# A gate's modulation summed on GpSimd and spread by a product with ones, in a transformer kernel on one core

## What is computed

```python
def adaln(cvec, w, b):
    m = jax.nn.silu(cvec) @ w + b
    return jnp.split(m, 3, axis=-1)

h = rms_norm(x, pre_g[i]) * (1.0 + scale) + shift
hc = rms_norm(xc, pre_g[i]) * (1.0 + cscale) + cshift
...
x = x + gate * rms_norm(y, post_g[i])
if not last:
    xc = xc + cgate * rms_norm(yc, post_g[i])
```

## Time and profile before

| | |
|---|---|
| time, 3 runs | 805.94 us median (805.93 to 806.41) |
| profiled execution, its own time | 805.69 us |
| its span, first to last instruction | 803.7 us |
| TensorE busy | 789.2 us |
| DVE, ScalarE busy | 505.1 us, 393.8 us |
| GpSimd busy | 42.9 us |

### The profile page before, as it was taken

How to read it: one execution, slowest core, us unless ns; L and a number is a source line. 1 busy time by engine, 2 the same in 40 slices (tenths; PEclk the granted TensorE clock), 3 DMA queues, 4 the chain that set the end, 5 groups by cost and what they waited for, 6 DMA issues and landing times. The chain is left out here.

```text
span 803.7 us, 11013 instructions
## 1 busy us (share of the span) xinstructions
PE 789.2 (98%) x4108; PEld 626.2 (78%) x4108; DVE 505.1 (63%) x873; ACT 393.8 (49%) x728; POOL 42.9 (5%) x55
## 2 busy tenths in 40 slices
PE   9999999999999999999999999999999999999998
PEld 5577787777777778777778877887788888888886
DVE  3474545225768776669856667799887645556454
ACT  3541323235878673575636646735245533343431
POOL 0120000000001001002100001300000000000000
PEclk9999999999999999999999999999999999999999
DMA  9974552355000037337432016883216655466521
GB/s 338 388 239 153 210 192 80 147 210 200 11 1 1 1 119 275 105 105 274 172 105 75 31 64 211 300 308 125 79 53 210 208 180 187 158 201 214 176 91 52
DMA packets 71303, 125.56 MB, mean 156 GB/s; under 512 B 2714, under 2 KB 28652, under 8 KB 71124
## 3 DMA queue, kind: packets, MB, share of 16 engines
q1 hardware_dynamic: 70208, 122.47, 43.8%
q0 software_dynamic: 512, 1.18, 0.5%
q10 hardware_dynamic: 532, 1.21, 0.5%
HBM read 123.79 MB, written 1.06 MB: 155 GB/s over the span
## 5 line engine op out<-in xcount | busy, mean ns | idle before, releaser
L822 PE MATMUL psum<-w_hi,act_hi 128*128 128x512 f32 (+1 forms) x712 | 289.6, 407 | 3.0 <-DVE w_lo L1973 1.0
L823 PE MATMUL psum<-w_lo,act_hi 128*128 128x512 f32 (+1 forms) x752 | 291.9, 388 | 0.0
L824 PE MATMUL psum<-w_hi,act_lo 128*128 128x512 f32 (+1 forms) x712 | 276.8, 389 | 0.0
L1948 DVE TENSOR_TENSOR w_lo<-raw,w_hi 128x2048 fp32r<-128x2048 f32 (+1 forms) x70 | 157.9, 2262 | 103.5 <-ACT w_hi L1369 103.4
L1369 ACT ACTIVATE w_hi<-raw 128x2048 fp32r<-128x2048 f32 (+1 forms) x74 | 139.9, 1895 | 71.2 <-PE psum L824 36.6
L822 PEld LDWEIGHTS psum<-w_hi,act_hi 128*128 128x128 f32 x712 | 133.7, 188 | 45.8 <-issue 17.3
L823 PEld LDWEIGHTS psum<-w_lo,act_hi 128*128 128x128 f32 x752 | 141.6, 188 | 25.4 <-issue 1.0
L824 PEld LDWEIGHTS psum<-w_hi,act_lo 128*128 128x128 f32 x712 | 133.7, 188 | 28.6
L1916 POOL TENSOR_TENSOR rstd<-ms,half_neg 128x1 f32<-128x1 f32 (+3 forms) x38 | 36.3, 957 | 557.6 <-DVE ms L1989 557.6
L1526 ACT ACTIVATE sc<-psum,nmax 128x512 f32<-128x512 f32 (+1 forms) x64 | 36.7, 585 | 24.2 <-DVE nmax L2196 24.2
L1451 ACT ACTIVATE sc<-psum 128x512 f32<-128x512 f32 (+1 forms) x62 | 32.4, 525 | 16.2 <-PE psum L925 8.7
(11 more groups left out here) (272 smaller groups left out, 991.1 us busy)
## 6 DMA issues: line engine op xcount, KB each, us to landing
raw<-in_a_w_in SPq DMA_DIRECT2D x16, 1024.0 KB, 9.8
raw<-in_ada_w SPq DMA_DIRECT2D x16, 1024.0 KB, 5.3
raw<-in_w_out SPq DMA_DIRECT2D x12, 1024.0 KB, 5.1
raw<-in_w_gate SPq DMA_DIRECT2D x22, 512.0 KB, 4.1
raw<-in_w_up SPq DMA_DIRECT2D x22, 512.0 KB, 5.2
raw<-in_w_down SPq DMA_DIRECT2D x11, 1024.0 KB, 5.0
raw<-in_b_w_in SPq DMA_DIRECT2D x10, 1024.0 KB, 7.7
raw<-in_w_in SPq DMA_DIRECT2D x10, 1024.0 KB, 5.9
```

Of the source, the lines that this page charges most:

```text
L822: pe.matmul(oh, x_hi, hi, start=(k == 0), stop=False)
L823: pe.matmul(o[:, 0:n], x_hi, lo, start=False, stop=False)
L824: mm = pe.matmul(oh, x_lo, hi, start=False, stop=(k == KT - 1))
L1948: ins = dve.tensor_tensor(rest, weights, hi.bitcast(F32), ALU.subtract)
```

## The change

The four gate parts are no longer multiplied on TensorE. GpSimd takes them from the raw ring: `gate_block` multiplies row block k by the block's column of silu (a value for each partition) and adds it to a total of 128x512. The totals, one for each part and condition, lie in `gate0`, and the product in `scaled`. A half is released (`s_sumused`) with its last product. `gate_row` then multiplies the total by a 128x128 matrix of ones, which adds up the partitions and spreads the sum. In the first projection the blocks stand behind GpSimd's small loads, in the second between its powers. The gate rows of in1 come after (1, 1) and (2, 2). The four pairs "norm1c" get banks 4 to 7. post_g of layer 0 is loaded by SP into kT with the other loads of that place and no longer by GpSimd. `sel` shrinks to two columns, `taken` moves into memory that another buffer shares. The diff, without these last declarations:

```diff
-BESIDE_IN0 = {(0, 3): ("ada0g", 0), (1, 1): ("ada0g", 1)}
-BESIDE_IN0.update({(2 + c, 1 if c < 3 else 0): ("ada1", c) for c in range(4)})
+BESIDE_IN0 = {(2 + c, 1 if c < 3 else 0): ("ada1", c) for c in range(4)}
 COLUMNS_IN0 = {(2 + c, 3 if c < 3 else 2): c for c in range(4)}
-BESIDE_IN1 = {(0, 0): 4, (1, 1): 5}
-GATE_IN1 = {(1, 0): 0, (2, 1): 1}
+SUMMED = [("ada0g", 0, (0, 1)), ("ada0g", 1, (0, 1)), ("ada1", 4, (0,)), ("ada1", 5, (0,))]
+GATE_IN1 = {(1, 1): 0, (2, 2): 1}
...
@@ -79,6 +80,8 @@
         for t in range(NT):
             if (c, t) in BESIDE_IN0:
                 plan += both(*BESIDE_IN0[(c, t)])
+        if c < 2:
+            plan += both("ada0g", c)
     for stage, chunks in (("out0", 2), ("in1", 5), ("out1", 2), ("in2", 6), ("out2", 2)):
         for c in range(chunks):
...
@@ -218,14 +221,13 @@
         put(("out0", 1, XT + t), 6 + t)
     norm("norm1")
     units("in1", range(3))
+    put(("gate1", 0, 0), 6)
     for pair in range(HALF_KT):
-        put(("norm1c", pair), 4 + pair % 2)
+        put(("norm1c", pair), 4 + pair)
     for c in range(3):
         for t in gemm_tiles("in1", c):
             put(("turn1", c, t), 2 + t)
-    for c in range(2):
-        put(("ada1", 4 + c, 0), 6 + c)
-        put(("gate1", 0, c), 6 + c)
+    put(("gate1", 0, 1), 7)
     for p in range(XT * HEADS):
         put(("s1", p), 2 + p % 2)
         put(("t1", p), 6)
...
+        def gate_sum(stage, c, s):
+            part = c if stage == "ada0g" else c - 4
+            return gate0[:, s, part * COLS:(part + 1) * COLS]
+        sum_no = {key: n for n, key in enumerate((stage, c, s) for stage, c, conds in SUMMED for s in conds)}
         def mod_rows(l, c):
             if l == 0:
                 return mrow[:, c * COLS:(c + 1) * COLS]
-            return sc[:, 5 + c % 2, :] if c < HALF_KT else mrow0g[:, (c - 4) * COLS:(c - 3) * COLS]
+            return sc[:, 5 + c % 2, :]
         k_flat = kT[:].rearrange("p h n -> p (h n)")
         gain2, gain3 = gate0[:, 1, :], q_flat[:, D:2 * D]
...
@@ -562,8 +572,11 @@
         emptied, firsts = {}, 0
+        summed_halves = [(stage, c, h) for stage, c, _ in SUMMED for h in range(2)]
         for n, (stage, c, h) in enumerate(loads):
-            if not stage.startswith("ada"):
+            if (stage, c, h) in summed_halves:
+                emptied[n] = (s_sumused, summed_halves.index((stage, c, h)) + 1)
+            elif not stage.startswith("ada"):
                 emptied[n] = released[half_no[(stage, c, h)]]
             elif h == 0:
                 firsts += 1
@@ -645,6 +658,7 @@
                     load(k_flat[:, 0:D], a["ada_b"][0, 2 * D:3 * D].partition_broadcast(P), s_par1)
                     load(k_flat[:, D:2 * D], a["ada_b"][1, 2 * D:3 * D].partition_broadcast(P), s_par1)
                     load(k_flat[:, 2 * D:3 * D], a["post_g"][1].partition_broadcast(P), s_par1)
+                    load(k_flat[:, 3 * D:4 * D], a["post_g"][0].partition_broadcast(P), s_par1)
                 if loads[n] == ("out1", 0, 0):
                     sp.wait_ge(s_res, NT)
...
@@ -855,18 +869,18 @@
                 name = (f"mod{l}", c)
                 o = begin(name)
                 for blk in range(HALF_KT):
-                    mm = pe.matmul(o[:, 2 * blk:2 * blk + 2], rows[:, blk * P:(blk + 1) * P], sel[:, :, 0],
+                    mm = pe.matmul(o[:, 2 * blk:2 * blk + 2], rows[:, blk * P:(blk + 1) * P], sel[:],
                                    start=True, stop=True)
                 mm.then_inc(bank_full(name), 1)
             def gate_row(l, s, c):
-                rows = mod_rows(1, 4 + c) if l else mrow0g[:, c * COLS:(c + 1) * COLS]
-                pe.wait_ge(*moved(("ada1", 4 + c, 0) if l else ("ada0g", c, 0)))
+                key = ("ada1", 4 + c, s) if l else ("ada0g", c, s)
+                pe.wait_ge(s_ones, 1)
+                pe.wait_ge(s_summed, sum_no[key] + 1)
                 name = (f"gate{l}", s, c)
                 o = begin(name)
-                pe.matmul(o, sel[:, s, :], rows,
-                          start=True, stop=True).then_inc(bank_full(name), 1)
+                pe.matmul(o, ones[:], gate_sum(*key), start=True, stop=True).then_inc(bank_full(name), 1)
             def norm(stage, ks=range(KT)):
                 tiles = norm_tiles[stage]
@@ -1073,9 +1087,6 @@
                     turn(("turn1", *units[n - 2]), 4 if units[n - 2][0] < 2 else 2)
                 if n == len(units):
                     gemm_unit("in1", 3, 0, ks=range(0, 5))
-                if n < len(units) and units[n] in BESIDE_IN1:
-                    for h in range(2):
-                        ada_half("ada1", BESIDE_IN1[units[n]], h)
                 if n < len(units) and units[n] in NORM_IN1:
                     norm("norm1c", NORM_IN1[units[n]])
                 if n < len(units) and units[n] in GATE_IN1:
...
@@ -1930,6 +1935,38 @@
                              (w_ukv[:, 0, :], a["w_uk_2"][0]), (w_ukv[:, 1, :], a["w_uv_2"][0]),
                              (relb[:], a["rel_bias_2"])):
                 pool.dma_start(dst, src).then_inc(s_late, 16)
+            def gate_block(stage, c, conds, k):
+                n = load_no[(stage, c, k // HALF_KT)]
+                if k % HALF_KT == 0:
+                    pool.wait_ge(landed[n % RAW], landed_at[n])
+                w = raw_view(n)[:, k % HALF_KT, :]
+                for s in conds:
+                    total, value = gate_sum(stage, c, s), cols[:, 8 * s + k:8 * s + k + 1]
+                    pool.wait_ge(*seq.last)
+                    used = s_sumused if k % HALF_KT == HALF_KT - 1 and s == conds[-1] else s_g
+                    seq.note(pool.tensor_scalar(scaled[:] if k else total, w, value, None, ALU.mult).then_inc(used, 1), used)
+                    if k:
+                        done = s_summed if k == KT - 1 else s_g
+                        pool.wait_ge(*seq.last)
+                        seq.note(pool.tensor_tensor(total, total, scaled[:], ALU.add).then_inc(done, 1), done)
+            pool.wait_ge(s_cst, 1)
+            for stage, c, conds in SUMMED[0:2]:
+                for k in range(KT):
+                    gate_block(stage, c, conds, k)
+            powers_through(("norm1", 2))
+            pool.wait_ge(s_res, NT - 1)
+            for key, (stage, c, conds), ks in ((("qk1", 0, 0), SUMMED[2], range(0, 3)), (("qk1", 0, 1), SUMMED[2], range(3, 5)),
+                                               (("post0", 3), SUMMED[2], range(5, KT)), (("qk1", 1, 0), SUMMED[3], range(0, 2)),
+                                               (("norm1", 3), SUMMED[3], range(2, 4)), (("qk1", 1, 1), SUMMED[3], range(4, KT))):
+                powers_through(key)
+                for k in ks:
+                    gate_block(stage, c, conds, k)
             powers_through(("ka", XT - 1))
             powers_through(("norm3", XT - 1))
...
@@ -2415,8 +2453,6 @@
                     if (c, t) == (0, 1):
                         post_mean(0, 3)
                         residual(0, 3)
-                    elif (c, t) == (1, 1):
-                        gates1(0)
                     return
                 r, buf = rs(key), sc[:, 5 + n % 2, w * P:2 * w * P] if t < XT else rot_buf(nm)
                 dve.wait_ge(s_vals, t + 1)
```

More of the change, by code:

```diff
@@ L316, in block_kernel @@
             rest_q = parts.enter_context(nc.sbuf_tensor("rest_q", [P, NT * HEADS, P], F32R))
+            taken = parts.enter_context(nc.sbuf_tensor("taken", [P, XT, 256], F32R))
         xs = sb("xs", [P, NT, D])
@@ L326, in block_kernel @@
         zbuf = sb("zbuf", [P, NT, D])
+        scaled = sb("scaled", [P, COLS])
         gate0 = sb("gate0", [P, 2, D])
@@ L330, in block_kernel @@
         ident_r = sb("ident_r", [P, P], F32R)
-        taken = sb("taken", [P, XT, 256], F32R)
         vecs = sb("vecs", [P, P])
@@ L335, in block_kernel @@
         cstat = sb("cstat", [P, KT, 32])
-        sel = sb("sel", [P, 2, P])
+        sel = sb("sel", [P, 2])
+        ones = sb("ones", [P, P])
         mod = sb("mod", [P, 2, 2, KT, 2])
@@ L437, in block_kernel @@
         s_res, s_yret = sem("residual_ready"), sem("retention_head_done")
-        N_CIN, N_VEC, N_LATE = 3, 4, 10
-        mrow0g = gate0[:, 0, :]
+        s_sumused, s_summed, s_ones = sem("summed_half_used"), sem("gate_sum_ready"), sem("ones_ready")
+        N_CIN, N_VEC, N_LATE = 3, 4, 9
+        def gate_sum(stage, c, s):
+            part = c if stage == "ada0g" else c - 4
+            return gate0[:, s, part * COLS:(part + 1) * COLS]
+        sum_no = {key: n for n, key in enumerate((stage, c, s) for stage, c, conds in SUMMED for s in conds)}
         def mod_rows(l, c):
@@ L1510, in unit0 @@
                     stage, part = BESIDE_IN0[before]
-                    if stage == "ada0g":
-                        move(mrow0g[:, part * COLS:(part + 1) * COLS], (stage, part, 0))
-                    else:
-                        move(mod_rows(1, part), (stage, part, 0), wait_for=("mod1", part - 2) if part >= 2 else None)
```

(15 more changed lines are left out.)

## The result

The changed kernel takes **889.76 us**, median of 4 runs (889.63 to 890.77), against 805.93 for the kernel before beside it: a ratio of 1.1042, interval 1.1022 to 1.1061. It is 83.8 us slower, where 18.7 was forecast; the range ended at 845. The profiled execution has a span of 887.8 us.

The account below looks back on a forecast made before the run. The prediction took TensorE, busy 98% of the span, as the bound, fed through a ring of six raw buffers. First projection +8.5, second +11.2 and banks -1.0 made +18.7 on 805.69: 824.4 us, range 799 to 845.

Parts of the forecast that it names:

- Product 0.54 us, addition 1.08: GpSimd's assumed time per 128x512 operation in both projections, from a memset's growth per column, doubled for the addition.
- upper pair: Dearer GpSimd prices, from a power's fixed cost plus the memset's slope: product 0.86 us, addition 1.32.
- Blocking 13.4 us: First projection: DVE's two-input time, four splits and five pairs of rotation ends, charged to GpSimd's sums.
- Rival 2: No blocking between DVE and GpSimd, operations at 0.54 and 1.08: 806.5 us, either side of no change; chance 0.12.
- First projection +8.5: Net us there: TensorE 12.6 late for chunk 3's second half, held by GpSimd in the ring, less 4.1 saved.
- Second projection +11.2: TensorE's wait for chunk 2's second half, ready at 395.6 against use at 384.40, the 4.0 saved already included.
- costs nothing more: Second projection: the gate's product on TensorE adds no wait, its sum being there by 387.
- Late powers 0 to 6: Second projection: GpSimd's last blocks delay tile (2,0)'s powers, 0 to 6 us; taken as nothing, hidden by another delay.
- Banks -1.0: Second projection: the fourth pair of context's transposes no longer waits for a bank, 1.0 us gained.
- Four parts, -8.1: Four gate parts leave TensorE, 2.0 us each, 8.1 in all, about 4.1 in each projection.
- Slow operations: Rival 3: GpSimd's operations at 0.86 and 1.32 us, late powers costing 6: 851 us; chance 0.15.
- Rival 1: GpSimd keeps up, averaging under 0.8 us per operation, blocking included: 802.2 us, 796.6 at best; chance 0.18.

Follow-up runs that it names:

- product_tt: Changed kernel with GpSimd's product written as an operation with two tensor inputs, the value broadcast along the row: 866.08 us.
- spaced: Kernel before with only the first projection's two gate parts on GpSimd, two-input product, loaded behind chunks 1 and 6: 807.54 us.
- free_raw: Changed kernel, but GpSimd reads ones instead of the raw halves, and a half counts as released once landed: 835.56 us.
- one_part: Kernel before with gate part 0 alone on GpSimd, two-input product, loaded behind the first projection's chunk 1; part 1 on TensorE: 803.48 us.
- attn: Kernel before with gate part 0 alone on GpSimd, two-input product, loaded behind the first projection's last chunk and summed beside attention: 807.77 us.
- second_alone: Kernel before with the change in the second projection alone, four banks included; first projection's gate parts on TensorE: 839.57 us.
- power_first: second_alone with the power of (2, 0) ahead of GpSimd's last four blocks and that of (2, 1) ahead of the last two: 831.14 us.
- banks_row: Kernel before with the four banks for context's features and the second gate row after tile (2, 2), nothing else: 809.07 us.
- awake: Kernel before with the first projection's change and four banks, plus matmuls on old data where TensorE stands longest: 862.43 us, against 862.39 without those matmuls.
- both_mended: Changed kernel with the two-input product and the powers of (2,0) and (2,1) ahead of GpSimd's last four row blocks: 865.02 us.

## Why the prediction was wrong

**In the first projection the mechanism held and its sizes did not; in the second the path was wrong.** SP's loads stood behind GpSimd in the order forecast, chunk 2's two halves and chunk 3's, and nothing after; TensorE stood for w_lo there. Of the 65.1 us between forecast and result, about 41.8 are the first projection (50.3 in place of 8.5) and 23.4 the second with its banks (33.6 in place of 10.2).

- *Product 0.54 us, addition 1.08.* This step failed most. Measured 1.56 and 1.27 undisturbed. Both prices came from how a memset grows with columns, which reads nothing. For 32 products and 28 additions that is 85.5 us in place of 47.5. The choice between two readings of the earlier trace rows, the memset's 0.9 ns a column and the power's 0.16 us, was made by what seemed alike; the measured 1.56 for 512 columns is over three times the memset's slope and a fiftieth of the power's, and my upper pair, 0.86 and 1.32, covered the addition and not the product. The estimate by the Trainium skill (GPSIMD Engine Reference, Elementwise side-by-side cycle accounting), 1.12 for the addition, was 12% low: near. That a product with one tensor input costs more than an addition with two is against its rule of thumb (the same page, Engine selection, calls one-input work "roughly line-rate" and only two-input work slow), and product_tt shows that it is the form of the instruction: the same product took 1.04 with two inputs.
- *Blocking 13.4 us.* GpSimd was busy 94.1 us between 55.9 and 155.7, 8.6 more than 85.5: less than forecast, in a longer stretch, because DVE now stood for the ring as well (67.5 us before its splits, from 54 to 180). In spaced, where DVE does not stand for the ring, the same 8.6 fall on 45.6 us (busy 43.2 against 34.6), close to the 13.4 in 60 that I had summed from the earlier trace rows. Rival 2, no blocking, falls by the product at 85.25. What I had not priced is the other direction: at nothing in the first projection in free_raw and one_part, at 1.2 us of waits there in spaced, and at 4.8 and 4.7 us in attention (attn, spaced).
- *First projection +8.5.* 50.3, and the chain of the prediction gives it when the sizes are put right. The second half of chunk 3 was released at 154.3 (the product at 152.69 ends), not 114.5: 37.8 later by the operations, 5.6 by 59 gaps of just under 0.1 that I had not priced, 1.2 by the later start, less 4.8 of blocking: 39.8. With the 9.6 of landing, rounding and split that is 163.9, and TensorE restarted at 163.79. So it is 12.6 + 39.8 - 4.1 = 48.3, and the low clock behind that last stall, 2 us, makes 50.3. The stalls before it (12.29 for chunk 2's *first* half, where the prediction had "some 2 us") are parts of the same sum, not additions to it.
- *Second projection +11.2, the sum "costs nothing more".* 33.6, by another road. The ring's hold was there and hidden (free_raw). The sum came at 393.2 on the clock of before (443.22 less 50.04, by which SP's loads of in1 had shifted, 396.58 for 346.54), not 387; and I compared it with TensorE's time of the next ring wait, though the gate's product stands before that in TensorE's order, at 378.6. 393.2 - 378.6 = 14.6. With the forecast's own 387 the product would have stood 8.4, so this is an error of the path and not only of a size. The sum of the stretch: 29.4 for the two long waits, 3.1 for w_lo and the rotation, some 5 of low clock behind them (an estimate from the granted clocks), less 4.1 for the parts and 1.0 for the old bank wait, 32.4; the last 1.2 is left open.
- *Late powers 0 to 6, taken at nothing.* 14.7. The shadow that was to hide it, the ring's wait at tile (2, 0), was 1.9 us long (until 451.18) and lay earlier in the chain, behind the sum's wait. second_alone less power_first prices the mending at 8.4.
- *Banks -1.0.* With the change's own row order about +3.1 (banks_row). The row of the wait was right; what was late next, DVE's act_lo, was not asked.
- *Four parts, -8.1.* Right: -4.2 for two in free_raw, -2.2 for one in one_part.
- *Rivals.* Slow operations (851) was the nearest and its prices were still too low. Rival 1 needed 0.8 us per operation, and 1.66 was measured with blocking and gaps (99.7 / 60); in its sum 54.7 + 32.4 is 87.1 and not 86, which changes nothing.

## What to carry to other kernels

Price an operation that the trace does not show by one that reads as much and writes as much, on the same engine and in the same form of instruction. When the nearest row reads nothing, its price is a lower bound, as the memset's 0.54 was for 1.56, and the range has to be open on the other side. When work moves to an idle engine, list in the order of the consumer every instruction that will wait for it, a ring's release, a sum, a bank behind a power, and price the first one reached. An idle engine that shares something with a busy one is only idle where the busy one has time in hand: the same part was worth 2.2 us in one stretch and cost 2 in another.

## What the runs showed of the hardware

- GpSimd at 128x512 in f32: product with a value per partition 1.56 us, the same product with that value broadcast as second input 1.04, addition 1.26 to 1.29, some 0.1 between operations that depend on each other.
- DVE with two inputs in SBUF and GpSimd at work on SBUF too: the one that begins second waits to the end of the first, on either engine (3.59 for 1.56, 1.55 for 0.43, 1.77 for 0.75). The Trainium skill states this (SBUF — State Buffer, Who interferes with whom: issue order decides who blocks), and these rows agree.
- After a stall of TensorE of 3.1 us (banks_row) the granted clock was at its lower level for about nine matmuls, 1.7 us of extra time; behind 12.3 us it was 2. In attn it was at 0.50 from 221 to 223 us, behind a stall of 1.68. In awake, with the stalls filled to 1.1 and 1.2 us, it stayed at 1.00, and with 3.7 and 2.7 left it fell.
- A wait of TensorE that was taken away was not given back whole: 12.1 us for a bank in power_first brought 8.4, and 6.8 in both_mended about 1.
